# The first projection behind a split: one weight unit over eight tiles, instead of two units in step

## The reference

```python
def first_block(x, mem, ...):              # two layers
    for l in range(2):
        h = _rmsnorm(x, norm_mix[l])
        x = x + mixer(h)                   # l=0: HGRN2 + convolution, l=1: MoBA attention + SGU
        x = x + _cross_attention(_rmsnorm(x, norm_xattn[l]), mem_n, ...)
        x = x + _swiglu(_rmsnorm(x, norm_ffn[l]), ffn_w_in[l], ffn_w_out[l])
    return _rmsnorm(x, final_norm)
def second_block(x, ...):
    h = _layer_norm(x, ln_in_g, ln_in_b)
    proj = h @ w_in                        # differential attention and RWKV-7 branches, gates
    h = _layer_norm(ALPHA * h + merged @ w_out, ln1_g, ln1_b)
    ffn = (silu(h @ ffn_w_gate) * (h @ ffn_w_up)) @ ffn_w_down
    return _layer_norm(ALPHA * h + ffn, ln2_g, ln2_b)
def hybrid_layer(x, ...):                  # third block
    proj = rmsnorm(x, norm_g) @ w_in       # mLSTM, forgetting attention, multiscale pooling
    merged = sum(sigmoid(gate[n]) * (y[n] @ w_branch[n]) for n in range(3))
    return rmsnorm(x + merged @ w_out, final_g)
```

## Time and profile before

| | |
|---|---|
| median of 3 runs | 4287.34 us (4280.61 to 4287.8) |
| the profiled execution | 4290.35 us, its span 4288.6 us |
| granted TensorE clock, mean | 0.901 |
| TensorE busy | 3865.0 us, 90% of the span |
| ScalarE, VectorE, GpSimd busy | 1242.6, 1154.8, 1284.7 us |
| products of weight units (L262 to L264) | 11688 matmuls |

### The profile page before, as it was taken

One profiled execution on the slowest core, in us unless ns is written; L12 is line 12 of the kernel. 1 busy time (PEld: TensorE's weight loads), 2 busy tenths in 40 slices (PEclk: granted clock), 3 DMA queues, 4 the chain that ended last, 5 costly groups with the idle time before them and its releaser, 6 DMA issues. The chain is left out here.

```text
span 4288.6 us, 40299 instructions
## 1 busy us (share of the span) xinstructions
PE 3865.0 (90%) x17052; PEld 3076.8 (72%) x17052; DVE 1154.8 (27%) x1807; ACT 1242.6 (29%) x1870; POOL 1284.7 (30%) x531
## 2 busy tenths in 40 slices
PE   7768999999889999988988788999989989999987
PEld 6657778787576787864867676787867758747866
DVE  2942310121322201114272224201154040031232
ACT  3323322233233322232331112322243412222232
POOL 2324234433042444320430001344414304403433
PEclk9879999999889999986997678899979979979998
DMA  3212122222021222220221002222212202202221
GB/s 116 69 49 89 59 85 97 91 82 81 1 99 59 92 95 93 84 85 0 77 92 41 1 1 96 69 98 89 98 59 89 84 0 94 98 5 69 99 95 67
DMA packets 82702, 305.40 MB, mean 71 GB/s; under 512 B 8885, under 2 KB 10713, under 8 KB 81242
## 3 DMA queue, kind: packets, MB, share of 16 engines
q1 hardware_dynamic: 78256, 280.61, 19.3%
q10 hardware_dynamic: 4266, 22.21, 1.3%
HBM read 291.77 MB, written 11.02 MB: 71 GB/s over the span
## 5 line engine op out<-in xcount | busy, mean ns | idle before, releaser
L2171 POOL TENSOR_TENSOR WL<-RW,WH 128x1024 fp32r<-128x1024 f32 x527 | 1284.5, 2442 | 2971.1 <-ACT WH L257 2970.9
L262 PE MATMUL PS<-XH,WH 128*128 128x512 f32 x2968 | 1174.7, 396 | 107.1 <-POOL WL L2171 60.8
L263 PE MATMUL PS<-XL,WH 128*128 128x512 f32 x2968 | 1168.0, 394 | 0.0
L264 PE MATMUL PS<-XH,WL 128*128 128x512 f32 x2968 | 1166.8, 393 | 0.0
L262 PEld LDWEIGHTS PS<-XH,WH 128*128 128x128 f32 x2968 | 566.1, 191 | 238.4 <-POOL WL L2171 62.3
L257 ACT ACTIVATE WH<-RW 128x1024 fp32r<-128x1024 f32 x527 | 550.2, 1053 | 495.8 <-PE PS L264 372.4
L264 PEld LDWEIGHTS PS<-XH,WL 128*128 128x128 f32 x2968 | 565.1, 190 | 119.5
L263 PEld LDWEIGHTS PS<-XL,WH 128*128 128x128 f32 x2968 | 566.3, 191 | 117.2 <-issue 0.2
L262 PE MATMUL PS<-YH,WH 128*128 128x512 f32 (+1 forms) x928 | 358.1, 386 | 67.7 <-POOL WL L2171 32.5
L263 PE MATMUL PS<-YL,WH 128*128 128x512 f32 (+1 forms) x928 | 355.9, 383 | 0.0
L264 PE MATMUL PS<-YH,WL 128*128 128x512 f32 (+1 forms) x928 | 355.0, 383 | 0.0
(11 more groups left out here) (404 smaller groups left out, 3524.1 us busy)
## 6 DMA issues: line engine op xcount, KB each, us to landing
RW<-in_units SPq DMA_DIRECT2D x527, 512.0 KB, 3.2
spill<-X ACTq DMA_DIRECT2D x2, 2048.0 KB, 6.5
X<-spill ACTq DMA_DIRECT2D x2, 2048.0 KB, 8.4
X<-in_xT SPq DMA_DIRECT2D x1, 2048.0 KB, 9.9
A<-spill ACTq DMA_DIRECT2D x1, 2048.0 KB, 11.2
out_T<-X ACTq DMA_DIRECT2D x1, 2048.0 KB, 7.4
spill<-X ACTq DMA_DIRECT2D x1, 1536.0 KB, 5.1
spill_gates<-X ACTq DMA_DIRECT2D x1, 1536.0 KB, 6.1
```

Of the source, the lines that this page charges most:

```text
L262: mm(out, hi, xh, start=first, stop=False)
L263: mm(out, hi, xl, start=False, stop=False)
L264: return mm(out, lo, xh, start=False, stop=last)
L2171: nc.gpsimd.tensor_tensor(WL[:, u % SPLIT, :], RW[:, u % RAW, :], WH[:, u % SPLIT, :].bitcast(F32), ALU.subtract).then_inc(split_done, 1)
```

## The change

In the two layer classes `pe_start` gets a list of one unit, and `pe_tile` begins with unit 1 instead of 2:

```diff
@@ Linear.tensor
-                    pe_start(pe, st, self.ready, self.u0, self.e0, [(self.xh, self.xl), (self.xh, self.xl)], self.cols)
-                    first = 2
+                    pe_start(pe, st, self.ready, self.u0, self.e0, [(self.xh, self.xl)], self.cols)
+                    first = 1
@@ Pairs.tensor
-                    pe_start(pe, st, self.ready, self.u0, self.e0, [self.yh or (XH, XL), (XH, XL)])
-                    first = 2
+                    pe_start(pe, st, self.ready, self.u0, self.e0, [self.yh or (XH, XL)])
+                    first = 1
```

## The result

The changed kernel takes 4305.51 us (median of 5 runs, 4305.09 to 4308.41) against 4287.34 us: ratio 1.0046, 95% interval 1.0035 to 1.0057. It is slower, as forecast, and the time lies in the range (4290 to 4306), at its very end. The ratio is worth 19.7 us where 9.7 were forecast: the size is off by a factor of two. The two medians lie 18.2 us apart. The profiled execution took 4305.27 us, its span is 4303.5 us, 14.9 more than before; the profiled execution of before (4290.35 us) lay 3.0 us above its own median, and that is the rest of the 18.2.

The account below looks back on a forecast made before the run. TensorE was taken as the bound. Norms +11.1, t.out +1.4, queries -1.9 and l0.glu -0.8 summed to +9.8 us, 4297 us on the median of 4287.34, with a range of 4290 to 4306.

Parts of the forecast that it names:

- What one unit alone changes at a norm: Six norm-fed places: third unit starts 14.6 us after the first matmul, 15.2 behind layer norms; +11.1 us together.
- The waits: TensorE's waits on the low part behind a norm: from 9 to some 30, growing by 8 to 15 us.
- Plain splits: Places without a norm: zero cost at all but t.out, since TensorE never catches up with the tiles.
- Its term: t.out: TensorE idles behind its first tile and the clock may rise later; +1.4 us, range +0.7 to +2.05.
- What it gives back: -1.9 us for the 0.94 us waits at x0.q and x1.q, -0.8 us at l0.glu's fourth unit.
- At l0.glu -0.5 instead of -0.8: Fourth unit of l0.glu: table loaded in the meantime, so its wait goes; -0.8 us, bounds -0.8 and 0.
- The sum: All changed places: 11.1 + 1.4 - 1.9 - 0.8 = +9.8 us, the shift carried on by TensorE.
- The second rival: Clock falls in the thinner stretch at the norms, second unit starts at half clock: 4306 to 4314 us; chance 0.08.
- the other bounds: Limits of the terms at t.out, queries and l0.glu; with norms at 7.2 to 14.4 us, sum +5 to +13.5.
- One sign of being wrong: In the profile after: a shift at a norm that is gone again before the next one.
- "same": Time within 0.2%, chance 0.37; its rival: late clock rises at most norms, +5 to +8.5 us, 4292 to 4296, chance 0.36.

Follow-up runs that it names:

- the parts alone: Kernel before with one unit at only the six norm-fed places (1.0037), the nine plain splits (1.0005), or x0.q and x1.q (0.9987).
- the delay experiment: Kernel before, old order, with overwritten matmuls added at the head of l1.qk's third unit: seven gave ratio 1.0014, ten gave 1.0007.
- the second profile: The changed kernel measured and profiled once more, nothing altered: ratio 1.0035 to the kernel before.
- fs.up alone: Kernel before with one unit first at fs.up only, two in step elsewhere: ratio 1.0012.
- the one with three matmuls added: Changed kernel with three more matmuls at the head of l1.qk's third unit: ratio 1.0034 to the kernel before.
- the repeat of the queries: Kernel before with one unit first at x0.q and x1.q only, measured a second time: ratio 0.9999.
- queries alone: Kernel before with one unit first at x0.q and x1.q only, two in step elsewhere: first measured ratio 0.9987.

## Why the prediction was right in direction and wrong in size

**What one unit alone changes at a norm: right, nearly to the digit.** 14.6 and 15.2 us were forecast for the stretch to the third unit, 14.5 and 15.1 were measured in every kernel and profile with one unit there; the sum of the six is 10.6 instead of 11.1 (9.5 to 10.6 against all traces of the old order). That the end can be read off without the clock was right too: the granted clock ranges from 0.81 to 0.84 at f0.up, l1.qk and f1.up and is 0.84 and 0.90 at the layer norms, and the length doesn't move; at l0.glu the clock rose some 3 us later than before, and the place took 14.5 us as well.

**The waits: too many counted.** I expected some 30 waits and 8 to 15 us more, and got 23 and 4.2 more. The printed idle is what lies between printed durations, and at full clock that hides 0.17 us of each hole (0.40 printed, 0.23 from start to start), 2.4 us for the fourteen new ones. Even with it the waits come to less than I expected.

**Plain splits: right.** Seven places at zero (l0.out as well, by the parts alone), and t.out a loss. Its term was +1.4, bounds 0.7 and 2.05; it is 2.3, just outside. The windows of t.out show a clock of 0.73 instead of 0.81, so (1 - 0.73) x 2 x 15.74 = 8.5 us at half instead of 5.1: the rise was put off by 3.4 us, more than the 2.7 I took as the most. The 2.3 hold for this pair of traces. With the old order t.out took 13.4 to 13.5 us in four traces and 12.4 to 12.5 in four others; with one unit 15.7 in three and 14.7 in the fourth. The cost there is so anything from 1.2 to 3.3 us.

**What it gives back: right.** 1.23 us instead of 0.94 at each query; the idle of a row leaves out what the slow first matmul costs. At l0.glu -0.5 instead of -0.8, and one statement was wrong: the table load is not issued ahead of the wait. The timeline of the changed kernel has it behind TensorE:

```profile
53.07 1.28 ACT L381 ACT_TABLE_LOAD   x1 [1.63 <-PE PS L264]
54.36 0.60 ACT L381 ACTIVATE SG<-PS 128x512 f32<-128x512 f32 x1
```

Before it stood at 51.75 us because ScalarE was busy until then (eight operations of L956, 49.16 to 51.73 us). What was saved is the time that ScalarE was late, not the load.

**The sum: the step that failed** is the sentence "TensorE stays the bound behind each of them, since the delayed third unit carries all that follows it; I see no slack that takes the shift up". The terms of the changed places add up to +10.0 where I had +9.8. What failed is the term for everything behind the changed places, put at nothing: between the two profiles it is +4.9 us net, the attention stretch alone +5.4 (133.6 to 139.0 us, 51.1 to 64.8 at half clock). A shift does not travel unchanged. In that stretch TensorE is busy in pieces and the clock goes down and up, five times in one trace and six in the other, and the delay experiment shows that this depends on the moment it begins. The same blindness is in the bounds: I let two executions differ only in how late the clock rises at the changed places, and looked for a falling clock only there. The second rival was right in kind and wrong in place. At the changed places of this trace the clock rose once and did not fall again before the third unit. The largest piece was lost one to two hundred microseconds behind l1.qk, in a stretch that the diff does not touch.

The bounds also hold a slip: with 14.4 us for the six places the other bounds (2.05, -1.9 and 0) give +14.5, not +13.5. From 4287.34 us that is 4301.9, and 4305.5 lies above it. The time falls into the stated range only because its upper end was set by the second rival, which did not occur; that is luck. One sign of being wrong did come up in this profile, a shift that is gone before the next norm: of the 1.8 us at l0.glu, 0.2 were left at the end of x0.ka. In the second profile it was still 1.8, so that was the execution and not the kernel.

Why did "same" (0.37) not come true? It needed late rises at most places and a sum of +5 to +8.5; the changed places gave +10.0, and the unchanged stretches came on top. The medians' 18 us are 8 above the changed places' 10, and the profile's own 5 above; the other 3 are where the profiled execution of before lay. The second measurement of the changed kernel, 1.0035, is worth 15 us, and the kernel before had medians of 4291.5, 4290.1 and 4287.7 us when it was measured beside the experiments. The excess over the forecast is so 5 to 10 us, and its exact size is open. Both profiles of the changed kernel show the same pieces, and the delay with the old order reproduces the largest, so for the attention stretch it is shown that a later start alone lengthens it. For t.gif it is shown that the change at fs.up alone brings the 2.2 us with it; that the moment is the reason is argued. For the mLSTM stretch it is argued only: kernels with about 19.6 us between the clock's last change and t.v's end took 213.8 to 214.0 us and those at 18.9 to 19.0 took 217.6, but one more kernel at 18.9, the one with three matmuls added, took 224.4, and two at 26.8 to 26.9 took 219.6 and 217.1, so this distance alone doesn't decide it.

What stays open is how much of the loss would be left if every unchanged stretch fell as well as before. By the traces it is 10 us, 1.0023. No kernel was found that shows it as a time.

## What to carry to other kernels

Where a layer begins while its input is still being made, compare the tile's interval with TensorE's time per tile for one unit and for several; two units in step turn a wait into work, and the gain is what the single unit would idle behind the first tile, here 1 to 3 us each. Where the input is ready, a start that waits for two units waits for one too many.

A shift of a microsecond or two in a kernel whose TensorE clock goes up and down is not carried through as it is. Before such a kernel is judged, compare the unchanged stretches of the two traces with their instruction counts and granted clock; if they differ, the comparison holds a piece that isn't the change's own work. A second profile of the same kernel shows which pieces repeat, and a variant with a small delay and the old order shows what the moment alone can do.

## What the runs showed of the hardware that I had not expected

The same 437 matmuls in the same order, with the same work of the other engines, took 131.5 to 143.2 us in the twelve traces of ten kernels, beginning 108.2 to 110.9 us behind the clock's last rise; 47.8 to 78.5 us of it were at half clock. The relation has no simple slope: 133.6 us at 108.6, 143.2 at 109.5, 139.0 at 110.2, 134.4 at 110.9. Nor is it the distance alone: the stretch took 131.5 us at 108.2 in the kernel with fs.up alone and 134.3 at 108.2 in the repeat of the queries, 135.9 at 110.6 and 134.5 at 110.7. What else enters is open.

It repeated in the changed kernel: two executions agreed to 0.1 us over that stretch, though they entered it 3.2 us apart. Two executions of the kernel with queries alone were 0.7 us apart. At the places in step the last matmul of the pair depends on when the clock rose, so the program falls into step with the clock there. One unit ends when the tiles end, 14.5 us after it began whatever the clock does, and so arrives elsewhere. That this is what parts the two groups of the table is my reading of it; shown is that the distance, made by a delay with the old order, gives the same stretch.

VectorE's low part is held up where it begins while GpSimd is splitting a unit. Of the 88 low parts of the plain splits (L652) 82 took at most 0.69 us in the kernel before; six began inside an instruction of GpSimd and took 1.67 to 2.86 us, and each of them ended 0.55 us behind the end of GpSimd's. The kernel after has the same six. At l1.out, t.br1 and t.br2 it hits only the first tile, for which TensorE waits anyway; at t.out the first two took 1.67 and 2.86 us, and that is what makes t.out the one plain split at which the change costs.
